# Gate blocks in four quarters of the array, later in their unit, and two branch products moved in the last recurrence

## The reference, cut to what matters

```
xc = causal_dwconv(xa, ...)                      # 4 taps, per channel
r  = sigmoid(blockdiag(wa) xc + ba)              # 16 blocks of 64 x 64
i  = sigmoid(blockdiag(wx) xc + bx)
log_a = -8 r softplus(-lambda);  a = exp(log_a)
u  = sqrt(-expm1(2 log_a)) * i * xc
h_t = a_t h_(t-1) + u_t                          # scan over time
branch_a = (h * gelu(ga)) @ w_br_a
branch_b = att @ w_br_b
merged = sigmoid(gate_a) * branch_a + sigmoid(gate_b) * branch_b
```

## Time and profile before

| | us |
|---|---|
| median of 3 runs | 1228.91 (1226.37 to 1229.41) |
| the profiled execution, its own time | 1226.24 |
| its span, first to last instruction | 1224.5 |
| mean granted clock of TensorE | 0.994 |

### The profile page before, as it was taken

One profiled execution on the slowest core, in us unless ns is written; L12 is line 12 of the kernel. 1 busy time (PEld: TensorE's weight loads), 2 busy tenths in 40 slices (PEclk: granted clock), 3 DMA queues, 4 the chain that ended last, 5 costly groups with the idle time before them and its releaser, 6 DMA issues.

```text
span 1224.5 us, 21256 instructions
## 1 busy us (share of the span) xinstructions
PE 1197.7 (98%) x8821; PEld 1164.1 (95%) x8821; DVE 660.8 (54%) x1337; ACT 462.6 (38%) x716; POOL 159.4 (13%) x258
## 2 busy tenths in 40 slices
PE   9999999999999999999999999999999999999996
PEld 6999999999999999999999999999999999999995
DVE  6543443534622346565645457888437884288721
ACT  6434434444333356666433344222212222122221
POOL 2264143152140000000100000000100001000031
PEclk9999999999999999999999999999999999999998
DMA  8566235245232222222253222322222322222221
GB/s 239 138 182 168 81 111 153 75 133 132 75 93 70 70 70 85 71 70 65 64 174 91 66 66 77 86 86 86 85 76 86 86 84 77 86 86 79 77 86 49
DMA packets 178980, 117.14 MB, mean 96 GB/s; under 512 B 6932, under 2 KB 170920, under 8 KB 178888
## 3 DMA queue, kind: packets, MB, share of 16 engines
q1 hardware_dynamic: 167456, 87.34, 25.3%
q0 software_dynamic: 11440, 28.79, 8.5%
q10 hardware_dynamic: 10, 0.01, 0.0%
HBM read 107.66 MB, written 8.45 MB: 95 GB/s over the span
## 4 chain that ended last, share of the span: by engine, by line
PE 95%; DVE 2%; ACT 2%; issue 1%; POOL 0%; ACTq 0%; POOLq 0%; DVEq 0%
PE ps L619 63%; PE ps L598 19%; PE ps L749 2%; PE ps L826 1%; PE ps L687 1%; PE ps L713 1%; PE ps L674 1%; PE ps L699 1%; PE ps L727 1%; PE ps L754 1%; PE ps L873 0%; PE ps L641 0%; PE ps L890 0%; DVE x_tok L1327 0%; PE ps L901 0%
## 5 line engine op out<-in xcount | busy, mean ns | idle before, releaser
L619 PE MATMUL ps<-h,w_s 128*128 128x288 f32 x3840 | 515.9, 296 | 0.0
L619 PEld LDWEIGHTS ps<-h,w_s 128*128 128x128 f32 x3840 | 510.6, 188 | 1.2 <-issue 0.2
L946 ACT ACTIVATE w_s<-w_raw 128x1024 fp32r<-128x1024 f32 (+1 forms) x161 | 167.4, 1040 | 381.7 <-PE ps L619 381.4
L1311 DVE TENSOR_TENSOR w_s<-w_raw,w_s 128x1024 fp32r<-128x1024 f32 (+1 forms) x161 | 192.5, 1195 | 197.6 <-ACT w_s L946 196.8
L598 PE MATMUL ps<-w_s,h 128*128 128x384 f32 x1152 | 216.7, 341 | 1.3 <-DVE h L1341 0.8
L598 PEld LDWEIGHTS ps<-w_s,h 128*128 128x128 f32 x1152 | 199.5, 189 | 3.2 <-issue 1.7
L619 PE MATMUL ps<-g_hi,w_s 128*128 128x288 f32 x768 | 136.1, 297 | 1.6 <-DVE g_lo L1745 1.6
L619 PEld LDWEIGHTS ps<-g_hi,w_s 128*128 128x128 f32 x768 | 113.4, 189 | 1.9 <-ACT g_hi L1275 1.8
L619 PE MATMUL ps<-g_lo,w_s 128*128 128x288 f32 x384 | 82.1, 295 | 0.0
L552 POOL DMA_DIRECT2D out<-f_row x12 | 6.2, 515 | 507.5 <-ACT f_row L1282 507.5
L619 PEld LDWEIGHTS ps<-g_lo,w_s 128*128 128x128 f32 x384 | 61.8, 188 | 0.0
(11 more groups left out here) (284 smaller groups left out, 1435.9 us busy)
## 6 DMA issues: line engine op xcount, KB each, us to landing
w_raw<-in_w_in SPq DMA_DIRECT2D x65, 512.0 KB, 4.0
w_raw<-in_w_up SPq DMA_DIRECT2D x48, 512.0 KB, 3.9
w_raw<-in_w_down SPq DMA_DIRECT2D x24, 512.0 KB, 3.8
kc<-in_cache_k_g POOLq DMA_DIRECT2D x48, 128.0 KB, 3.0
vc<-in_cache_v_g POOLq DMA_DIRECT2D x12, 512.0 KB, 5.9
w_raw<-in_w_br_a SPq DMA_DIRECT2D x8, 512.0 KB, 3.8
w_raw<-in_w_out SPq DMA_DIRECT2D x8, 512.0 KB, 3.8
x_tok<-in_x_prompt SPq DMA_DIRECT2D x4, 512.0 KB, 7.9
```

The source lines that it names most:

```text
L619: last = mm(pu[u % 2][:, 512 * a:512 * a + HALF], w[:, part, k, :], x[:, k, HALF * a:HALF * (a + 1)], start=(k == 0 and i == 0), stop=(k = ...
L946: A(w_s[:, ring(u), 0, 0:nkt[u], :], w_raw[:, u % NRAW, 0:nkt[u], :], ACT.Copy).then_inc(hi_ready, 1)
L1311: TT(w_s[:, ring(u), 1, 0:nkt[u], :], w_raw[:, u % NRAW, 0:nkt[u], :], w_s[:, ring(u), 0, 0:nkt[u], :], ALU.subtract).then_inc(lo_ready, 1)
```

## The change

The gate weights wa and wx are kept as 64-blocks only: [P, KT, 64] in place of [P, KT, 128] with zeros, so their memsets go. wa's two blocks lie on the partitions of their inputs; wx's are swapped. A copy xsw of xc with its two halves of 64 partitions exchanged is made by two transfers on GpSimd's queue, from SBUF to SBUF. `gate_products` then has eight calls of 64 x 64 blocks in place of four of 128 x 128, each block in another quarter of the array, waits for xsw too, and stands ahead of row block 7 of the third unit in place of row block 1. In `recur(7)` the branch product 0 is taken ahead of the scan, and the low split of w_br_b's unit 3 and branch product 1 between the scan and the l_y products; ScalarE's y_part(7) moves one w_br_b step later.

```diff
--- before.py
+++ after.py
@@ -35,6 +35,7 @@
 C_SM = C_PM + 9 * P
 C_N = C_SM + 4 * P + NG * NS
 
+LB = 64
 STRIP, SLOTS = 32, 2
 DIA = SLOTS * P + NT * SLOTS
 
@@ -242,8 +243,10 @@
 
 
         sg_a = at(o_r, "sg_a", [P, KT, TOK])
-        wa = at(o_r + VEC, "wa", [P, KT, P])
-        wx = at(o_r + VEC + 4 * KB, "wx", [P, KT, P])
+
+        wa = at(o_r + VEC, "wa", [P, KT, LB])
+        wx = at(o_r + VEC + 2 * KB, "wx", [P, KT, LB])
+        xsw = at(o_r + VEC + 4 * KB, "xsw", [P, LW])
         l_st = at(o_r + VEC + 8 * KB, "l_st", [P, KT, 36])
         l_row = at(o_r + VEC + 8 * KB + 1152, "l_row", [36, D])
         att_hi = at(o_a, "att_hi", [P, NH, TOK], F32R)
@@ -319,7 +322,7 @@
         vc_in = sem("vc_in")
         kcT_ps, kcT_used = sem("kcT_ps"), sem("kcT_used")
         kcT_rdy = [sem("kcT_rdy0"), sem("kcT_rdy1")]
-        gw_zero, gw_in = sem("gw_zero"), sem("gw_in")
+        gw_zero, gw_in, xsw_in = sem("gw_zero"), sem("gw_in"), sem("xsw_in")
         l_link, xa_pad, xc_rdy, gate_ps, l_gr, gate_read = (sem(x) for x in ("l_link", "xa_pad", "xc_rdy", "gate_ps", "l_gr", "gate_read"))
         as_rdy, aa_rdy, a2_rdy, m2_rdy, mul_rdy, y_rdy, y_hi_rdy, y_lo_rdy = (sem(x) for x in ("as_rdy", "aa_rdy", "a2_rdy", "m2_rdy", "mul_rdy", "y_rdy", "y_hi_rdy", "y_lo_rdy"))
         lst_rdy, lst_ps, lrow_rdy, l_out = sem("lst_rdy"), sem("lst_ps"), sem("lrow_rdy"), sem("l_out")
@@ -514,19 +517,22 @@
 
 
             pool.wait_ge(unit_done, 1)
-            pool.memset(wa[:, :, :], 0.0).then_inc(gw_zero, 1)
-            pool.memset(wx[:, :, :], 0.0).then_inc(gw_zero, 1)
-            pool.wait_ge(gw_zero, 2)
-            for buf, name in ((wa, "lru_wa"), (wx, "lru_wx")):
+            for n, (buf, name) in enumerate(((wa, "lru_wa"), (wx, "lru_wx"))):
                 src = t[name][0].rearrange("(c j) d e -> j d c e", j=2)
                 for j in range(2):
-                    pool.dma_start(buf[64 * j:64 * j + 64, :, 64 * j:64 * j + 64], src[j]).then_inc(gw_in, 16)
+                    p0 = LB * (j ^ n)
+                    pool.dma_start(buf[p0:p0 + LB, :, :], src[j]).then_inc(gw_in, 16)
             pool.wait_ge(at_ready, 5 * NH)
             pool.wait_ge(at_lo_rdy, NH)
             for s in kv_out:
                 pool.wait_ge(s, 32 * NH)
             pool.memset(xa[:, :, 0:XPAD], 0.0).then_inc(gw_zero, 1)
             for c in range(KT):
+                pool.wait_ge(xc_rdy, c + 1)
+                if c:
+                    pool.wait_ge(gate_ps, c)
+                for j in range(2):
+                    pool.dma_start(xsw[LB * j:LB * (j + 1), :], xc[LB * (1 - j):LB * (2 - j), c % 2, :]).then_inc(xsw_in, 16)
                 pool.wait_ge(aa_rdy, c + 1)
                 if c:
                     pool.wait_ge(m2_rdy, c)
@@ -821,16 +827,21 @@
                 pe.wait_ge(xc_rdy, c + 1)
                 if c:
                     pe.wait_ge(gate_read, c)
-                for i, w in enumerate((wa, wx)):
-                    for a in range(2):
-                        last = mm(ps[2 + i][:, 512 * a:512 * a + LW // 2], w[:, c, :],
-                                  xc[:, c % 2, a * LW // 2:(a + 1) * LW // 2], start=True, stop=True)
+                pe.wait_ge(xsw_in, 32 * (c + 1))
+
+                for a in range(2):
+                    cols_ = slice(a * LW // 2, (a + 1) * LW // 2)
+                    for i, (w, x) in enumerate(((wa, xc[:, c % 2, :]), (wx, xsw[:, :]))):
+                        for j in range(2):
+                            rows, o = slice(LB * j, LB * (j + 1)), LB * (j ^ i)
+                            last = mm(ps[2 + i][o:o + LB, 512 * a:512 * a + LW // 2], w[rows, c, :], x[rows, cols_],
+                                      start=True, stop=True)
                 last.then_inc(gate_ps, 1)
 
             for c in range(KT):
                 unit(U_LRU + 3 * c, h_hi, h_lo)
                 unit(U_LRU + 3 * c + 1, h_hi, h_lo)
-                unit(U_LRU + 3 * c + 2, h_hi, h_lo, None, {1: lambda: gate_products(c)})
+                unit(U_LRU + 3 * c + 2, h_hi, h_lo, None, {7: lambda: gate_products(c)})
 
 
             with pe.Fori(0, KT // 2) as i:
@@ -1224,7 +1235,7 @@
             root(KT - 1)
             for m in range(1, KT):
                 hi_split(U_BB + m + 1)
-                if m == 1:
+                if m == 2:
                     y_part(KT - 1)
             for m in range(KT):
                 u = U_BA + m
@@ -1564,7 +1575,7 @@
                 link[0] += 1
                 dve.wait_ge(l_link, link[0])
 
-            dve.wait_ge(gw_zero, 3)
+            dve.wait_ge(gw_zero, 1)
 
             def conv(c):
                 u = U_LRU + 3 * c
@@ -1593,18 +1604,18 @@
 
                 STT(a_s[:, :], a_2[:, :], 1.0, a_s[:, :], ALU.add, ALU.mult).then_inc(m2_rdy, 1)
 
-            def recur(c, midway=()):
+            def recur(c, before_scan=lambda: None, after_scan=lambda: None):
                 dve.memset(pads(a_a[:, :]), 0.0)
                 dve.wait_ge(mul_rdy, c + 1)
                 linked(dve.memset(a_s[:, 0:1], 1.0))
                 linked(STT(l_u[:, :], g_i[:, :], 0.5, a_s[:, :], ALU.mult, ALU.mult))
                 linked(dve.tensor_copy(pads(l_u[:, :]), vt[:, c, V_H0:V_N]))
-                for u in midway:
-                    lo_split(u)
+                before_scan()
                 if c:
                     dve.wait_ge(lst_rdy, c)
                     dve.wait_ge(y_lo_rdy, c)
                 linked(dve.tensor_tensor_scan(l_h[:, :], a_a[:, :], l_u[:, :], 0.0, ALU.mult, ALU.add))
+                after_scan()
                 g_ = ga[:, c % 2, :]
                 taken(dve, U_LRU + 3 * c + 1)
                 TT(prompt(l_y[:, :]), in_classes(l_h[:, 0:SEQ]), prompt(g_), ALU.mult)
@@ -1654,10 +1665,10 @@
                 TT(mg_lo[:, m, :], sg_b[:, m, :], mg_hi[:, m, :], ALU.subtract).then_inc(mg_lo_rdy, 1)
 
             lo_split(U_BB + 1)
-            recur(KT - 1, (U_BB + 2,))
-            branch_b(0)
+
+            recur(KT - 1, lambda: (lo_split(U_BB + 2), branch_b(0)), lambda: (lo_split(U_BB + 3), branch_b(1)))
             y_rest(KT - 1)
-            for m in range(2, KT):
+            for m in range(3, KT):
                 lo_split(U_BB + m + 1)
                 branch_b(m - 1)
             dve.wait_ge(lst_rdy, KT)
```

## The result

The changed kernel takes 1232.3 us (median of 11 runs, 1227.33 to 1237.06), the kernel before 1227.83 (11 runs, 1224.63 to 1230.95). The ratio is 1.0039, with a 95% interval of 1.0026 to 1.0053: 0.4% slower, 3.2 to 6.5 us. I had forecast 1226.8, that is 2.1 us faster, and gave slower a chance of 0.27. The time lies inside my range of 1220.5 to 1233.5 and just above the likeliest case's own, 1223 to 1232; the change went the other way than forecast. Three executions took 1463 to 3014 us (one of act_queue, one of quarters_moves_x, one of the kernel before beside them); the medians further down contain them, the ratios and their intervals don't.

What follows compares the result with a forecast made beforehand. TensorE, busy 98% of the span, was taken as the bound. 1226.24 us profiled, - 1.2 (seven rounds) - 0.9 (block 0) + 0 (last recurrence) = 1224.1, or 1226.8 against the median; range 1220.5 to 1233.5.

Steps and rivals of the forecast that it cites:

- the likeliest case's own: The forecast case: copy between 2.93 and 3.98 us, quarters in parallel; range 1223 to 1232 us, chance 0.45.
- the chain of distances: Each recurrence round: steps behind a_s move 1.05 us forward; low splits arrive in time by 0.1 and 0.2 us.
- G + 16.72: G is the end of a block's gate products; the next block's conv output xc is ready 16.72 us later.
- The quarters: Gate products as 64x64 blocks, four at a time: 1.15 us a block, 0.87 less than before.
- where TensorE waits for xsw: Ahead of the gate products' new place: a wait of 0.70 us a round, bounds 0 and 1.4.
- rival C: Gate products: quarters go two at a time, 2.16 us a block, so 1232.2 us; C or worse, chance 0.15.
- its way of 3.16 us: From xc to TensorE's use of xsw: wake 0.28, two issues 0.53, landing 2.3, TensorE's wake 0.05.
- break-even of 3.33: Time from xc to xsw at which a round gains nothing; each 0.1 us beyond costs 0.7 us of the whole.
- Rival B: Slow copy, perhaps one half behind the other: 3.86 us way, TensorE waits 1.4 us, kernel 2.8 us slower; chance 0.12.
- I take 0: Last recurrence and branch products, w_br_b stretch: no net change, between +0.3 us and -0.4 us.
- The wait of 0.65 us: At the fifth w_br_b unit, whose accumulator waits for branch product 2 behind y_lo: some 0.65 us.
- the two cases that I had weighed in the prediction: Clock after the 2.6 us wait, w_br_b stretch: if it falls, +0.3 us; if it holds, -0.4 us.

Runs made afterwards that it cites:

- act_queue: Changed kernel with both xsw transfers issued by ScalarE behind its GELU in place of GpSimd; 1228.46 us against 1229.2 for the kernel before, ratio 0.9990.
- quarters_moves_x: Kernel before plus quarters without copy at row block 1, moved branch products and GpSimd's x loads held back; 1219.8 us against 1229.2, ratio 0.9932.
- no_copy: Changed kernel without copy, late place or new last recurrence; wx's blocks read xc, ScalarE takes g_i in two passes; 1222.86 us against the kernel before's 1229.2.
- two_queues: Changed kernel with xsw's lower half issued by GpSimd, upper by ScalarE, each with its own semaphore; 1231.57 us against the kernel before's 1228.25, ratio 1.0025.
- after_xlate: Changed kernel with GpSimd's five x loads held back until w_br_a's second unit is done; 1228.01 us against 1228.37 for the kernel before, ratio 1.0009.
- branch_xlate: Kernel before with moved branch products and GpSimd's x loads held back until w_br_a's second unit is done; 1223.58 us against 1229.2, ratio 0.9957.
- branch_only: Kernel before with only the two branch products moved as in the change; 1225.86 us, ratio 0.9983 to the kernel before.
- gates_only: Changed kernel with the last recurrence's order as before, so only gate blocks, copy and later place remain; 1231.8 us against the kernel before's 1228.37, ratio 1.0038.

## Why the prediction was wrong

**What bounds the kernel, and the chain of distances: right.** The a_s chain, the square root, the low split and the conv came where the earlier trace rows moved by 1.05 us puts them, to 0.15 us. I had xc at G + 16.72; here G is 490.15 and xc is done at 506.80, G + 16.65.

**The quarters: right in kind, and where TensorE waits for xsw right in size.** They run four at a time, so rival C is out, although wa's two row halves do write one bank at once, on different partitions: 1.17 us from the first of them to the next dense matmul, where I had 1.15. In a round without any wait (no_copy) the price is 1.37, because the matmuls at the seam, entering and behind, are further apart too. I had left that out: there the gain is 0.65 us a block, not 0.87. In the changed kernel it costs only block 0 its 0.22, since in the other seven rounds those 0.2 us lie inside the wait for xsw.

**The copy: the first failed step is its way of 3.16 us.** The wait is where I said and 0.84 us long, not 0.70 (21.39 - 19.18 - 1.37). The way from xc to TensorE is 3.52 us in the round shown and 3.56 on the mean of seven, not 3.16: in that round landing 2.54 for 2.3, TensorE's wake 0.14 for 0.05, GpSimd's 0.30 for 0.28. A round that waits is as long as the loop through the copy: 16.65 from the end of the gate products to xc, 3.56 for the way and 1.17 for the products make 21.38, where I had 16.72 + 3.16 + 1.15 = 21.03. So the way alone is 0.40 a round, which is more than the 0.36 that the round is too long, and more than the 0.17 that it was to gain. It lies past the break-even of 3.33 that I had named. Seven such rounds are 2.5 us and block 0 is 0.22; together they take the recurrence stretch from 2.1 us shorter, as forecast, to 0.7 longer. The biggest term in it is the landing, which I took from a store of 96 KB for want of a transfer from SBUF to SBUF. Rival B's mechanism decided it, though at a smaller size than B's 3.86. On the halves, the Trainium skill, "SBUF — State Buffer", section "Can I just issue two DMAs to hit both halves?", has two such transfers serialize. The traces agree in direction and not in size: with the issues 0.54 us apart the second transfer takes 0.1 us longer than the first, with 0.26 apart (two_queues) 0.4 on the mean, where serializing whole would be 0.7 by my estimate.

**The last recurrence: the step that failed is "I take 0".** The wait ahead of the second unit came as forecast (2.6), and the unit's end and branch product 0 came as worked out. The wait of 0.65 us that I had at the fifth unit came to 0.1. But I counted only TensorE, ScalarE and VectorE and wrote that nothing else on SP's queue moves. Two queues did move against each other. GpSimd's x loads wait for y_lo of block 7, which the inserted splits and branch products made later against the w_br_b units, while the w_br_a load comes with the sixth w_br_b unit's low split: 8.5 us apart before, 2.3 after. Then the load lands in 10.5 us (10.0 in the second execution), TensorE stands 2.7 us (2.1) and runs 3.4 at half clock. In place of 0 the w_br_b stretch cost 2.7 to 3.3 us; without the meeting it would have been 0.9 less than before (after_xlate, 35.44, whose clock didn't fall; for a clock that holds I had 0.4 less).

**The sum.** Forecast -2.1; recurrence +0.6 to +0.7 and w_br_b +2.7 to +3.3 make +3.4 to +3.9, inside the measured 3.2 to 6.5. These two stretches explain the miss. The rest adds 2.9 in the traces, for which the prediction had no term; with it the traces give 6.3 to 6.8, at the upper end. The profiled executions do differ by that much (1226.24 and 1232.58), but that the timed runs contain it isn't shown (last section).

**The change does contain a gain.** Its two ideas are worth 5.2 us in the recurrence stretch (quarters, as no_copy; 6.5 in the timed runs) and 4.3 in the w_br_b stretch (moved products, as branch_xlate; 5.3 in the timed runs). What ate them was the copy with the place that it forces, and the x loads.

## What to carry to other kernels

When a step is moved by some microseconds, list for every queue what is issued on its semaphores, and for each load what other load now starts beside it; a transfer that was hidden by distance alone is not hidden by design. A helper copy between partitions costs the whole way from producer to use (here 3.5 us for 2.5 of landing) and is worth avoiding by writing the output to other partitions and letting the engine that reads it move it back. When a forecast gain is tenths of a microsecond in each of many rounds, its sign hangs on the least certain term: here a landing taken from another kind of transfer, 0.3 us too short, against a gain of 0.17. And where an engine waits, ask which loop sets the round; a cost inside the wait doesn't lengthen it.

## What the runs showed that I had not expected

**The same matmuls at two paces.** In the first FFN stretch, from about 750 to 860 us, dense matmuls of 288 columns follow each other at 130.0 ns in some kernels and at 133.3 in others, with the granted clock at 1.00 in both. This makes the rest 578.4 or 581.3 us. The kernel before, the changed one and branch_only each gave the same value in two executions, and nothing in that stretch differs between them. That looks as if it belonged to the built kernel. But the same two paces stand in the w_br_b stretch, and there they change between executions of one kernel: the sixth and seventh w_br_b units take 3.12 us each in the changed kernel's first execution and 3.20 in its second, and in branch_only 3.20 in the first and 3.12 in the second. And the timed runs disagree about the 2.9 us. Against the kernel before, branch_only's two other stretches give -1.8 and -2.3 us, with the rest +1.2 and +0.7, where -3.9 to -0.2 is measured; two_queues gives +3.4, with the rest +6.3, where 1.2 to 4.9 is measured. Both speak against the rest. gates_only gives +2.4, with the rest +5.3, where 2.8 to 6.5 is measured, and speaks for it; the changed kernel and quarters_moves_x allow both. So whether the slow pace holds in the timed runs, and what sets it, stays open. It limits what can be said of 1 to 3 us in any comparison of these kernels.

**The clock after equal gaps.** After a gap of 2.6 us ahead of the second w_br_b unit the granted clock fell to 0.50 for 3.4 us in gates_only (at 604.5), act_queue, two_queues and the changed kernel's second execution, but not in its first and not in after_xlate. The same gap stands ahead of the third unit in no_copy (at 605.0) and in the kernel before (at 604.9); no_copy had no fall, the kernel before had one in both executions, and no_copy's stretch is 1.7 us shorter for it. In the changed kernel the fall costs less, 0.9 us up to the end of the fifth unit (20.1 against 19.1 from the stretch's start), since TensorE then waits less for branch product 0: the two cases that I had weighed in the prediction.

**A pass from one half of the partitions to the other.** ScalarE reading PSUM partitions 64 to 127 and writing SBUF partitions 0 to 63 takes 0.75 us for 600 columns, no more than the full-height pass (0.76 in the earlier trace rows).
